# Two-block transformer kernel, second mixer: where in VectorE's order a finished weight unit leaves PSUM

## The reference, cut to what matters

```
def mixer_fox_nsa(h, w_in, b_f, cmp_pe, cmp_w1, cmp_w2, w_out):
    proj = h @ w_in
    ...
    fq, fk, fv, ff, nq, kc, vc, ks, vs, kw, vw, ng = [proj[..., offs[i]:offs[i + 1]] for i in range(len(IN_SIZES))]
    log_f = jax.nn.log_sigmoid((ff + b_f).astype(jnp.float32))
    o_fox = fox_attention(fq.reshape(hd), fk.reshape(hd), fv.reshape(hd), log_f)
    ...
    o_nsa = nsa_attention(nq.reshape(B, S, NSA_HEADS, HEAD_DIM), kc.reshape(kvd), vc.reshape(kvd),
                          ks.reshape(kvd), vs.reshape(kvd), kw.reshape(kvd), vw.reshape(kvd),
                          gates, cmp_pe, cmp_w1, cmp_w2)
    return jnp.concatenate([o_fox, o_nsa], axis=-1) @ w_out
```

## Time and profile before

| | |
|---|---|
| median of 3 runs | 1684.82 us (1684.52 to 1685.41) |
| profiled execution: its time, and its span from first to last instruction | 1686.36 us, 1684.6 us |
| TensorE matmul busy | 1642.8 us, 98% of the span |
| VectorE busy | 880.2 us, 52% |
| ScalarE busy | 706.6 us, 42% |
| GpSimd busy | 166.6 us, 10% |
| mean granted TensorE clock | 0.992 of full speed |
| taking a unit out of PSUM (L1261) in `in_b` | 23 instructions, 594.8 to 821.3 us |

### The profile page before, as it was taken

One profiled execution on the slowest core, in us unless ns is written; L12 is line 12 of the kernel. 1 busy time (PEld: TensorE's weight loads), 2 busy tenths in 40 slices (PEclk: granted clock), 3 DMA queues, 4 the chain that ended last, 5 costly groups with the idle time before them and its releaser, 6 DMA issues.

```text
span 1684.6 us, 22206 instructions
## 1 busy us (share of the span) xinstructions
PE 1642.8 (98%) x8041; PEld 1357.0 (81%) x8041; DVE 880.2 (52%) x1443; ACT 706.6 (42%) x1179; POOL 166.6 (10%) x249
## 2 busy tenths in 40 slices
PE   8999999999999999999899999999999999999997
PEld 7676788888888888888777888888888788888887
DVE  5544557777743356667756544443227644444233
ACT  4545454444432226667646333323226622333221
POOL 2011000000000032445402000002000200000001
PEclk9999999999999999999999999999999999999999
DMA  5211222232332252121112322333331123232331
GB/s 181 79 45 39 75 88 97 91 99 100 100 100 92 96 127 72 42 64 51 51 61 77 100 89 98 100 99 90 99 101 51 51 100 93 94 100 88 104 108 51
DMA packets 57157, 144.86 MB, mean 86 GB/s; under 512 B 14160, under 2 KB 20976, under 8 KB 57088
## 3 DMA queue, kind: packets, MB, share of 16 engines
q1 hardware_dynamic: 55680, 141.58, 26.6%
q0 software_dynamic: 688, 1.26, 0.4%
q10 hardware_dynamic: 720, 1.10, 0.2%
HBM read 138.67 MB, written 2.10 MB: 84 GB/s over the span
## 4 chain that ended last, share of the span: by engine, by line
PE 91%; DVE 4%; ACT 3%; issue 2%; DMA 0%; POOL 0%; ACTq 0%; DVEq 0%
PE ps L1820 26%; PE ps L1822 26%; PE ps L1821 26%; PE ps L1991 1%; PE ps L2230 1%; PE ps L2245 1%; PE ps L2283 1%; PE ps L2231 1%; PE ps L1927 1%; PE ps L1925 1%; PE ps L1926 1%; PE ps L1981 1%; ACT whi L769 1%; PE ps L2044 0%; PE ps L2376 0%
## 5 line engine op out<-in xcount | busy, mean ns | idle before, releaser
L1820 PE MATMUL ps<-hhi,whi 128*128 128x512 f32 x1400 | 552.8, 395 | 4.8 <-DVE wlo L1233 4.4
L1822 PE MATMUL ps<-hhi,wlo 128*128 128x512 f32 x1400 | 546.4, 390 | 0.0
L1821 PE MATMUL ps<-hlo,whi 128*128 128x512 f32 x1400 | 546.0, 390 | 0.0
L1233 DVE TENSOR_TENSOR wlo<-raw,whi 128x1024 fp32r<-128x1024 f32 x234 | 286.7, 1225 | 468.8 <-ACT whi L769 466.0
L769 ACT ACTIVATE whi<-raw 128x1024 fp32r<-128x1024 f32 x247 | 261.3, 1058 | 559.8 <-PE ps L1822 559.4
L1820 PEld LDWEIGHTS ps<-hhi,whi 128*128 128x128 f32 x1400 | 263.2, 188 | 68.7 <-issue 8.2
L1822 PEld LDWEIGHTS ps<-hhi,wlo 128*128 128x128 f32 x1400 | 263.2, 188 | 55.7
L1821 PEld LDWEIGHTS ps<-hlo,whi 128*128 128x128 f32 x1400 | 263.5, 188 | 53.4 <-issue 1.2
L1820 PE MATMUL ps<-ahi,whi 128*128 128x512 f32 x480 | 186.7, 389 | 0.0
L1821 PE MATMUL ps<-alo,whi 128*128 128x512 f32 x480 | 186.7, 389 | 0.0
L1822 PE MATMUL ps<-ahi,wlo 128*128 128x512 f32 x480 | 186.7, 389 | 0.0
(11 more groups left out here) (345 smaller groups left out, 1888.0 us busy)
## 6 DMA issues: line engine op xcount, KB each, us to landing
raw<-w_up_b SPq DMA_DIRECT2D x88, 512.0 KB, 3.4
raw<-w_up_a SPq DMA_DIRECT2D x44, 512.0 KB, 3.4
raw<-w_in_b SPq DMA_DIRECT2D x23, 512.0 KB, 3.6
raw<-w_in_a SPq DMA_DIRECT2D x19, 512.0 KB, 3.5
raw<-w_down_b SPq DMA_DIRECT2D x16, 512.0 KB, 3.5
raw<-w_out_a SPq DMA_DIRECT2D x8, 512.0 KB, 3.5
raw<-w_down_a SPq DMA_DIRECT2D x8, 512.0 KB, 3.4
raw<-w_out_b SPq DMA_DIRECT2D x8, 512.0 KB, 3.8
```

What stands on the lines that cost most here:

```text
L1233: dve.tensor_tensor(wlow(n), raw[n % RAW][:, :], whigh(n).bitcast(f32), ALU.subtract).then_inc(lo_done, 1)
L1820: pe_.matmul(out, wh, hi, start=start, stop=False)
L1821: pe_.matmul(out, wh, lo, start=False, stop=False)
L1822: return pe_.matmul(out, wl, hi, start=False, stop=stop)
```

## The change

The two lines that take a unit out of PSUM at the end of VectorE's step move into the next step, behind its reciprocal, maxima and low parts, and ahead of its sums and conversions. TensorE's, ScalarE's, GpSimd's and SyncE's order stay as they are.

```
@@ -1713,6 +1713,8 @@
                                               ps[:, 2 + s % 2, 0:n * P].rearrange("p (j q) -> p j q", q=P),
                                               pth[:, j % 2, 0:n, s % 2, :].bitcast(f32), ALU.subtract
                                               ).then_inc(B["lo"], 1)
+                    for u in finished_at(p, k - 1) if k else []:
+                        evacuate(p, u, 0)
                     for o, (last, kind, t, c) in enumerate(FILLS):
                         if last + 4 == k:
                             dve.wait_ge(B["half"], o + 1)
@@ -1764,8 +1766,6 @@
                             dve.wait_ge(B["ohi"], j + 1)
                             dve.tensor_tensor(tile(hlo, m), tile(outf, m), tile(hhi, m).bitcast(f32), ALU.subtract
                                               ).then_inc(B["olo"], 1)
-                    for u in finished_at(p, k):
-                        evacuate(p, u, 0)
```

## The result

| | before | after |
|---|---|---|
| median of 4 runs each | 1684.91 us (1684.52 to 1685.41) | 1697.77 us (1695.78 to 1697.94) |
| ratio to before | | 1.0068, 95% interval 1.0054 to 1.0082 |
| profiled execution: time, span | 1686.36, 1684.6 us | 1697.94, 1696.2 us |

The change makes the kernel slower by 12.9 us by the medians. The forecast was 6.1 us, with a range up to 1696.0: the sign was right, the size half of what came, and the measured time lies outside the range.

A forecast was written before the change was run, and what follows sets the result against it. TensorE was taken as the bound; late blocks of 2.0 + 3.1 + 1.95 + 0.49 us, less 0.44 and 1.0 us given back, made 6.1 us on a median of 1684.82: 1690.9 us, range 1686.5 to 1696.

The forecast's parts named there:

- The place and the sign: TensorE's first block of the next unit waits for the evacuation at some 12 places, 0.5 to 1.6 us each; slower.
- the end gains: Unit 22, at the loop's end: TensorE's wait of 2.40 us shrinks by about 1.0 us.
- The rival that the maxima count more: VectorE's standstill and the scores' waits for maxima go, the end gains 1.0 us: 1680.6 us, faster; chance 0.06.
- the cost of waking: At each late block: TensorE's waking, about 0.1 us, set against VectorE's overlap between instructions, also about 0.1 us.
- the upper bound of the prediction: High end, +9.5 us: no give-back at units 14 and 18, no gain at the end, waking 0.1 us at 12 blocks.
- The give-back at units 14 and 18: Blocks 0.39 us late, then 0.61 us of maxima waits returned in the next step; net -0.44 us for both.
- the clock: Rival: half-clock stretches behind the waits at units 12, 16 and 20, some 1.7 us each: 1696 us; chance 0.08.
- The shorter standstills speak against it: Reason against the clock rival: TensorE's standstills shorter than 2.40 us; its new ones at units 12, 16, 20 reach 1.6 us.
- the case of no change: Rival: TensorE gets delays back in steps behind late blocks, leaving +3.1 us or less, about 1687.5 us; chance 0.11.
- GpSimd does not hold the evacuation: Rival claimed the opposite: GpSimd's subtraction holds the evacuation, 12 blocks some 0.8 us later, 1700 us; chance 0.03.

The follow-up runs named there:

- e1: Against the kernel before: evacuation moved into the next step behind the maxima but ahead of the low parts; 1679.44 us, ratio 0.9956.
- c0_change_again: The change itself, unaltered, measured again on another chip against the kernel before; 1699.07 us, ratio 1.0072.
- e3_again: The change plus eight unread matmuls in each of TensorE's waits at units 12, 16 and 20; 1694.47 us, ratio 1.0043 to before.
- e4: Against the kernel before: only units 12, 16 and 20 are evacuated behind the next step's low parts; 1694.59 us, ratio 1.0040.
- e6: Against the kernel before: all units but 12, 16 and 20 are evacuated behind the next step's low parts; 1690.45 us, ratio 1.0024.

## Why the prediction was wrong in size

**The place and the sign were right.** The low parts come when ScalarE lets them: 2.38 us behind the unit's last matmul at unit 13, before and after. The waits stand at the 12 places named, are longest at units 12, 16 and 20, the wait for maxima at the units is gone, and the end gains 0.97 us where 1.0 was forecast (its last product comes 10.0 us later in the span, where 5 to 6 were forecast, for the reasons below). The rival that the maxima count more is refuted for this place, and holds for the place of e1.

**The first step that failed, by 1.6 us in the sum of the waits, is the cost of waking.** "VectorE's overlap between instructions and TensorE's waking take about 0.1 us each (estimates) and are set against each other" took TensorE to be at full pace at once. The overlap is 0.09 us (713.09 to 713.00), waking 0.15, and then the second matmul starts 0.31 us behind the first instead of 0.23. At units 12, 16 and 20 the pair of low parts also lasted 1.18 instead of 1.15 us. That is some 0.1 us and more at each of 12 blocks, and the upper bound of the prediction held it.

**The give-back at units 14 and 18 came as described.** GpSimd's subtraction is out of the way, the conversions take 1.41 us, and the five matmuls behind unit 14 take 1.16 us instead of 1.76: 0.60 us came back where 0.61 was forecast. The term was 0.39 - 0.61 and measured 0.47 - 0.51, so that it gave nothing, because the block came later and restarted more slowly; that is the first step again.

**The second step that failed, and the largest, is the clock, which the sum put at nothing: 4.6 us by the medians of c0_change_again and e3_again, 3.2 in the table.** It stood in the prediction as a rival by itself with a chance of 0.08, all three places or none. "The shorter standstills speak against it" was too weak a reason: the trace before had one wait of 2.40 us with a fall behind it and one of 1.86 without, at 862.59 in the layer behind the loop, which the prediction did not read. What the runs show is a risk per wait. In the 12 traces, waits of TensorE of 1.79 to 2.55 us between 640 and 900 us are 33; directly behind 15 of them the clock falls to 0.50, and behind 4 others (all at step 42) it falls some 6 to 7 us later. Behind the loop's shorter new waits, up to 1.4 us, it did not. That the rival's price of 5.1 us comes near to 4.6 is luck: in the profile after, one of its three places had a fall, and the other new fall lies behind the loop. In hindsight, a term of three waits at half of 1.6 us each would have given 2.4 us more; with the waking, the forecast would have been within 3 us of the measured time.

**The two other rivals.** TensorE gets nothing back but what stands in the table, so the case of no change is out. GpSimd does not hold the evacuation: 0.68 us under its subtraction. The Trainium skill, GPSIMD Engine Reference, Specifications, puts the contention on instructions of VectorE in a 2-port mode or with two operands in SBUF; the traces agree as to the operands, since the conversions were held (2.48 us for two) and the evacuation, with one operand in PSUM, was not.

## What to carry to other kernels

An instruction that waits on an engine has two kinds of dependants: those queued behind it, and those that need its result. Before it is moved back, read from the timelines when each of them becomes urgent, and move it past the first kind only as far as the second allows; here the place behind the maxima is worth 8 us and the place behind the low parts costs 13. A new standstill of the engine that bounds the kernel has a price beyond its length, for the restart and for the clock, and a split that is moved later to help one queue moves the engine behind it too.

## What the runs showed of the hardware that was not expected

The clock does not answer to the length of one wait by itself. The wait of 1.84 to 1.86 us for a low part in the layer behind the loop stands in all 12 traces, and the clock falls behind it in five of them (the profile after, c0_change_again, e1_behind_maxima, e4 and e6) and not in the other seven; each fall costs some 1.6 us. What else decides it these traces do not show. Two kernels with the same waits can therefore differ by such steps, and a difference of 1.6 us in one trace says little about the edit between them.

TensorE restarts slowly after a wait, with no fall of the clock in it: 0.15 us from the end of the evacuation to the block, and 0.30 to 0.31 us instead of 0.23 to the next matmul, at each of the 47 waits for the evacuation of over 0.9 us in these traces.
